# Half the columns of the second expert table read once as tiles instead of gathered row by row

## The chip, the cores and the metric

One core of one Trainium2 chip runs the whole program in one launch. The metric is the device time of that core in microseconds. A core has TensorE (PE), VectorE (DVE), ScalarE (ACT), GpSimd (POOL) and SyncE (SP), each with its own instruction queue, and 16 DMA engines that all queues share.

## The reference, cut to what matters

Two transformer blocks over 256 tokens of width 2048, in float32. The first and most of the second are products with weight matrices, attention and scans; the change leaves them as they are. It concerns the last layer, a mixture over 16384 single-row experts:

```python
def peer(x, w_q, sub_keys, expert_u, expert_v):      # tables: 16384 x 2048
    q = (x @ w_q).reshape(B, S, PEER_HEADS, 2, PEER_HALF)
    s = jnp.einsum('bshpk,hpnk->bshpn', q, sub_keys)  # 8 heads, 2 sides, 128 keys
    top_s, top_i = lax.top_k(s, PEER_TOPK)            # 16 of 128 on each side
    ...                                               # 16 best of the 16 x 16 sums
    ids = jnp.take_along_axis(cand_i, pos, axis=-1)   # first key * 128 + second key
    g = jax.nn.softmax(best_s, axis=-1)
    ...
        u = jnp.take(expert_u, it, axis=0)
        act = jax.nn.gelu(jnp.einsum('td,tkd->tk', xt, u)) * gt
        v = jnp.take(expert_v, it, axis=0)
        return jnp.einsum('tk,tkd->td', act, v)
```

So each token picks 8 x 16 = 128 experts. It needs 128 rows of the first table for 128 dot products, and 128 rows of the second, weighted and added. A last RMS norm follows.

## The kernel before, in words

Tokens lie on the 128 partitions, in two blocks t = 0 and 1. Up to about 2110 us weights stream through three buffers (`raw`): SP loads them, ACT makes a rounded copy (`wh`, line 1779), DVE the rest (`wl`, line 2222), and PE multiplies rounded parts (lines 1523 to 1536).

The expert phase numbers its work n = 0 to 255, where n = 128 t + k is pick k of every token in block t. For each n:

- POOL issues an indirect DMA of 128 rows of 8 KB, one for each token, from the first table into one of four buffers `Ub` (`get_u`, line 2784), once the dot that used the buffer is done;
- DVE multiplies the buffer with the normalised tokens `xn` and sums (`dot`, line 2656);
- after each four dots ACT applies gelu (`weigh`, line 2056) and DVE multiplies by the softmax weight (`weigh`, line 2663);
- POOL gathers 128 rows of the second table into one of twelve buffers `Vb` (`get_v`, line 2795);
- ACT builds a diagonal matrix of the 128 activations (`spread`, line 2064), and PE multiplies it with the rows and adds into four PSUM banks (`spread`, line 1685), in plain float32.

Between the dots DVE also chooses the experts of the 16 pairs (t, head): `top_sides`, `top_pairs`, `top_ids` and `top_weights` (lines 2598 to 2648). A planner, the class `Plan`, fixes the order of every engine's instructions before the program is written. It keeps one clock per engine, charges each piece of work an estimated time (`put`) and takes the option that could start first (`products`, line 881). It charges 2.55 us for a dot, 2.49 us of DMA for any gather, and 3.6, 2.4, 3.1 and 1.0 us for the four parts of a choice. Its order is then static: each engine runs its list in order and waits on semaphores. When the last rows are in, `finish` and `close` (lines 2675 and 2694) add the sums to the residual `X`, and normalise and store it.

Two queues matter for the change. POOL's holds the gathers in the planned order, so a gather that waits for its buffer holds those behind it. ACT's holds gelus and diagonals, and DVE's `weigh` waits for the gelu while all later dots stand behind it.

## Time and profile before

| | us |
|---|---|
| Median of three runs (lowest, highest) | 3402.46 (3401.48, 3403.65) |
| Profiled execution, first to last instruction (span) | 3401.7 |
| PE busy over the span | 3122.3 (92%) |
| DVE busy | 2242.8 (66%) |
| ACT busy | 1261.4 (37%) |
| POOL busy | 558.9 (16%) |
| HBM read | 931.5 MB |

The profiled execution has no time of its own beside its span; the span is 0.8 us below the median of the runs. Busy shares are means over stages with different limits, so the prediction reads stages. In the windows view, a row gives a stretch, its length, then for each engine the busy time and the number of instructions, then the granted TensorE clock, the mean busy share of the 16 DMA engines, and GB/s. A float32 product of PE shows as two records, a rounded one (float32r) as one.

### The profile page before, as it was taken

What the parts mean: (1) busy time and instruction counts of PE and PEld (TensorE: products, weight loads), DVE (VectorE), ACT (ScalarE), POOL (GpSimd) and SP (SyncE); (2) the same over time, 40 slices, a digit from 0 to 9 for tenths busy, and PEclk for the clock granted to TensorE, in tenths of its full rate; (3) what the DMA queues carried; (4) which work ended last, traced back from release to release, by engine and by line L of the source; (5) the groups of instructions that cost most, each with busy time, mean ns of one, the idle gap of its engine ahead of it and who ended that gap; (6) DMA issues with size and microseconds to landing.
All of it is one profiled execution on the core that took longest, in us unless ns stands there. A gap on an engine that the chain in (4) does not pass through costs nothing.

```text
span 3401.7 us, 35002 instructions
## 1 busy us (share of the span) xinstructions
PE 3122.3 (92%) x13582; PEld 2276.3 (67%) x13582; DVE 2242.8 (66%) x3449; ACT 1261.4 (37%) x1848; POOL 558.9 (16%) x533
## 2 busy tenths in 40 slices
PE   8999999999999999999999999999787777777776
PEld 7998998888888888888888888844232222222222
DVE  7786777775566877786557775888864454444445
ACT  6554566554445555554446763111110010000001
POOL 0000000000000000000000000664444343333333
PEclk9999999999999999999999999999999999999999
DMA  6554555546555555555556567999999999999998
GB/s 233 164 149 158 158 177 168 179 161 203 185 182 185 186 186 185 189 186 206 186 195 207 177 232 271 387 420 427 427 427 427 427 426 427 427 427 427 427 427 363
DMA packets 405597, 935.87 MB, mean 275 GB/s; under 512 B 16472, under 2 KB 246521, under 8 KB 339129
## 3 DMA queue, kind: packets, MB, share of 16 engines
q0 software_dynamic: 75936, 547.39, 38.4%
q1 hardware_dynamic: 328482, 385.92, 34.4%
q8 instruction: 107, 1.75, 0.2%
q10 hardware_dynamic: 1016, 0.35, 0.0%
q14 instruction: 56, 0.46, 0.0%
HBM read 931.50 MB, written 2.10 MB: 274 GB/s over the span
## 4 chain that ended last, share of the span: by engine, by line
PE 65%; DMA 27%; DVE 6%; issue 1%; ACT 1%; POOL 1%; POOLq 0%; DVEq 0%; SPq 0%; ACTq 0%
DMA Ub<-in_peer_u,ids 26%; PE W L1526 14%; PE W L1534 11%; PE W L1536 11%; PE W L1535 11%; PE W L1524 7%; DVE Ub L2656 4%; PE M L1685 2%; PE T L1685 2%; PE M L1587 1%; PE W L1460 1%; PE W L1523 1%; DMA Vb<-in_peer_v,ids 1%; POOL Vb L2795 0%; PE T L1421 0%
## 5 line engine op out<-in xcount | busy, mean ns | idle before, releaser
L2222 DVE TENSOR_TENSOR wl<-raw,wh 128x1024 fp32r<-128x1024 f32 (+1 forms) x720 | 850.6, 1186 | 563.5 <-ACT wh L1779 561.6
L1779 ACT ACTIVATE wh<-raw 128x1024 fp32r<-128x1024 f32 (+1 forms) x720 | 740.7, 1031 | 894.0 <-PE W L1536 573.6
L2656 DVE CUSTOM_DVE_ANT_0 Ub<-Ub,xn 128x2048 f32<-128x2048 f32 x256 | 585.6, 2291 | 480.9 <-DMA Ub<-in_peer_u,ids 480.9
L1526 PE MATMUL W<-u,wh 128*128 128x512 f32 x2040 | 722.7, 397 | 0.0
L1524 PE MATMUL W<-u,wl 128*128 128x256 f32 x2176 | 603.1, 282 | 0.2 <-DVE u L2184 0.2
L1685 PE MATMUL W<-Vb,diag 128*128 128x512 f32 x996 | 459.1, 603 | 156.7 <-DMA Vb<-in_peer_v,ids 154.2
L1685 PEld LDWEIGHTS W<-Vb,diag 128*128 128x128 f32 x996 | 179.4, 190 | 436.4 <-issue 373.8
L1526 PEld LDWEIGHTS W<-u,wh 128*128 128x128 f32 x2040 | 383.3, 188 | 88.4
L1534 PE MATMUL W<-wh,u 128*128 128x512 f32 (+1 forms) x1152 | 436.2, 379 | 1.2 <-DVE u L2582 1.0
L1536 PE MATMUL W<-wh,u 128*128 128x512 f32 (+1 forms) x1152 | 428.0, 371 | 0.0
L1535 PE MATMUL W<-wl,u 128*128 128x512 f32 (+1 forms) x1152 | 427.6, 371 | 0.0
L1524 PEld LDWEIGHTS W<-u,wl 128*128 128x128 f32 x2176 | 410.7, 189 | 6.4 <-issue 0.5
L2784 POOL DMA_INDIRECT Ub<-in_peer_u,ids x256 | 279.0, 1090 | 694.3 <-DVE dots L2656 588.0
L1685 PE MATMUL M<-Vb,diag 128*128 128x512 f32 x508 | 248.5, 612 | 95.5 <-DMA Vb<-in_peer_v,ids 93.1
L2056 ACT ACTIVATE dots<-dots 128x4 f32<-128x4 f32 x64 | 13.1, 205 | 782.6 <-DVE dots L2656 782.6
L2795 POOL DMA_INDIRECT Vb<-in_peer_v,ids x255 | 268.2, 1052 | 102.5 <-issue 71.0
L1685 PEld LDWEIGHTS M<-Vb,diag 128*128 128x128 f32 x508 | 91.2, 191 | 242.5 <-issue 209.0
L1685 PE MATMUL T<-Vb,diag 128*128 128x512 f32 x508 | 240.9, 597 | 0.0
L1534 PEld LDWEIGHTS W<-wh,u 128*128 128x128 f32 x1152 | 216.5, 188 | 30.5 <-issue 1.4
L1536 PEld LDWEIGHTS W<-wh,u 128*128 128x128 f32 x1152 | 216.2, 188 | 30.8
L1535 PEld LDWEIGHTS W<-wl,u 128*128 128x128 f32 x1152 | 216.6, 188 | 28.9
L1685 PEld LDWEIGHTS T<-Vb,diag 128*128 128x128 f32 x508 | 97.9, 193 | 124.3 <-issue 124.3
(371 smaller groups left out, 3265.0 us busy)
## 6 DMA issues: line engine op xcount, KB each, us to landing
raw<-in_w_in SPq DMA_DIRECT2D x128, 1024.0 KB, 5.2
raw<-in_w_up SPq DMA_DIRECT2D x88, 1024.0 KB, 4.8
raw<-in_w_down SPq DMA_DIRECT2D x44, 1024.0 KB, 4.9
raw<-in_w_in SPq DMA_DIRECT2D x144, 256.0 KB, 3.4
raw<-in_w_out SPq DMA_DIRECT2D x32, 1024.0 KB, 5.0
raw<-in_w_proj_a SPq DMA_DIRECT2D x16, 1024.0 KB, 4.9
Wb<-in_peer_w_q SPq DMA_DIRECT2D x16, 1024.0 KB, 7.7
raw<-in_w_proj_b SPq DMA_DIRECT2D x4, 1024.0 KB, 5.0
```

Of the source, the lines that this page charges most:

```text
L1460: m = q.matmul(pairs[n % 2][h][:, 0:T], w[:, k, col(h)], u5[:, kk, :], start=kk == 0, stop=kk == b.kt - 1)
L1524: i = q.matmul(pr[h][:, 0:T], vl, xh, start=False, stop=False)
L1526: i = q.matmul(o, vh, u[:, :, kk, :], start=False, stop=last)
L1534: q.matmul(o, th, H[:, k, :], start=first, stop=False)
L1535: q.matmul(o, th, L[:, k, :], start=False, stop=False)
L1536: i = q.matmul(o, tl, H[:, k, :], start=False, stop=last)
L1685: i = q.matmul(out_banks[t][j][:, :], diag[:, r % 4, :], v_row(n)[:, CK[j]], start=k == 0, stop=k == 127 or n == LAST_WHOLE and j > 1)
L1779: q.activation(wh[:, s % NS, 0:b.half], r, ACT.Copy).then_inc(s_hi, 1)
L2222: q.tensor_tensor(wl[:, s % NS, 0:b.half], r, wh[:, s % NS, 0:b.half].bitcast(F32), SUB).then_inc(s_lo, 1)
L2656: q.tensor_tensor_reduce(U[:, :], U[:, :], xn[:, t, :], 1.0, 0.0, MUL, ADD, dots[t][:, k:k + 1]).then_inc(s_dot, 1)
L2784: q.indirect_dma_start(Ub[place][:, :], None, eu, bass.IndirectOffsetOnAxis(ids[t][:, k:k + 1], 0)).then_inc(s_u[place], 16)
L2795: q.indirect_dma_start(v_row(n)[:, :], None, ev, bass.IndirectOffsetOnAxis(ids[t][:, k:k + 1], 0)).then_inc(s_v[n % NV], 16)
```

## The change

The second table's upper 1024 columns are still gathered row by row (half rows of 4 KB). Its lower 1024 columns are read once, in order, as 128 tiles of 128 experts x 1024 columns on SP's queue, and multiplied on PE by a matrix A of activations (experts x tokens), which is built on the chip.

- **Half gathers, block 0.** 128 gathers of upper halves (`get_v`), the first 72 through twelve places, the others through four, which lie where the scores were and wait for all choices. PE adds them by diagonals into two banks, as before.
- **Building A.** For each token, A[first key, second key] is the product of two one-hot matrices over its picks, the one weighted by the activations. Four tokens make a group; there are 32 groups for each block. `one_hot` and `spike` make the factors on ACT: an equality test against 0 to 127 is written as Abs (four operations of 128 columns), a wait, and Relu over 512 columns; the spike waits again and scales with four more. In block 1 every second spike is on DVE instead (four `tensor_scalar`). PE multiplies (`build`, four products of 128 columns), and ACT copies the bank to SBUF (`keep`). The groups of block 0 wait for all of its activations. The one-hots of block 1 follow, 28 of them at once and the last four after dot 235; its spikes wait for the activation of dot 239. The last 16 picks of block 1 are not in A.
- **The planner** gets an option "make" for these pieces, which is taken when ACT's clock plus 0.8 us is the earliest, and charges ACT 4.2 us for a one-hot with its spike, 0.6 for a keep, 1.5 for a one-hot alone and 2.3 for a spike alone. A dot from 240 on waits in the plan until a share of the spikes is placed. The first table has five buffers, of which four are in turn at a time (three from n = 236 on). A choice of experts is placed earlier than before where `eager` holds.
- **The products** (`dense`). For each tile j: ACT rounds the tile (`high`) and its 256 columns of A (one word in every 512 bytes for each token), DVE makes the rests (`low`, `low_a`), and PE does twelve rounded products of 512 columns. Each eleventh tile is multiplied in plain float32 with four products (`whole_tile`). Tiles have five buffers.
- **Aside.** Block 1's upper halves, and the lower halves of its last 16 picks, are 144 half gathers (`get_aside`, five buffers, not before the last dots), each added by DVE to `X` with one multiply-add of 1024 columns.
- The final norm's gain is multiplied in while the products run; both blocks close together.

The core of the diff (lists of places, semaphores and the closing steps are left out):

```diff
-NU = 4
-NV = 12
+NU = 5
 NW = 13
-LEAD = 7
 GROUP = 4
 LAG = 0.6
 
-ASIDE = (250, 252)
-HALVES = (253, 254, 255)
-SPREADS = [n for n in range(256) if n not in ASIDE]
-LAST_WHOLE = max(n for n in SPREADS if n not in HALVES)
+HALF = D // 2
+LATE = 16
+BUILT = 128 - LATE
+NE = 12
+NB = 4
+FIRST_ROWS = 72
+NT = 5
+NH = 3
+NA = 5
+ASIDES = 128 + LATE
+RAW = 11
...
+def row_place(m):
+
+    if m < FIRST_ROWS:
+        return m % NE, m // NE, m - NE if m >= NE else None
+    r = m - FIRST_ROWS
+    return NE + r % NB, r // NB, m - NB if r >= NB else None
...
+def whole_tile(j):
+    return j % RAW == RAW - 1
...
+    def build(self, i):
+
+        self.add("build", i)
+        self.put("PE", 1.0, max(self.clock["ACT"], self.clock["DVE"] if i % 2 and i > 32 else 0.0) + 0.2)
+        if i % 32:
+            self.keep(i - 1)
+
+    def keep(self, i):
+        self.add("keep", i)
+        self.put("ACT", 0.6, 0.0)
+
+    def make(self):
+
+        c = self.clock
+        yield lambda: None if 31 not in self.acted or FIRST_ROWS - 1 not in self.spreads else max(
+            self.acted[31], self.spreads[FIRST_ROWS - 1])
+        self.add("turn_ids", 0)
+        self.add("turn_act", 0)
+        self.put("ACT", 1.2, self.put("PE", 0.8, 0.0))
+        for i in range(32):
+            yield lambda: c["ACT"]
+            self.add("one_hot", i)
+            self.add("spike", i)
+            self.put("ACT", 4.2, 0.0)
+            self.build(i)
+        self.keep(31)
+        yield lambda: None if 124 not in self.dotted else self.when(("chosen", 1, 7), ("xn", 1, 3))
+        self.add("turn_ids", 1)
+        self.put("ACT", 0.6, self.put("PE", 0.6, 0.0))
+        for i in range(32, 64):
+            yield lambda: self.dotted.get(U_LAST[0]) if i >= 60 else c["ACT"]
+            self.add("one_hot", i)
+            self.put("ACT", 1.5, 0.0)
+        yield lambda: None if self.row_next < 128 else self.acted.get(BUILT // GROUP + 31)
+        self.add("turn_act", 1)
+        self.put("ACT", 0.6, self.put("PE", 0.4, 0.0))
+        for i in range(32, 64):
+            yield lambda: c["DVE"] if i % 2 else c["ACT"]
+            self.add("spike", i)
+            self.put("DVE" if i % 2 else "ACT", 0.8 if i % 2 else 2.3, 0.0)
+            self.build(i)
+            self.spiked = i - 31
+        self.keep(63)
...
+            eager = self.chosen < 3 + n / 9 and since > 0
+            if self.tasks and (dot is None or dot - c["DVE"] > 1.4 or 16 * self.chosen - u < 4 or eager):
+                options.append((c["DVE"] - (0.05 if eager else 0.0), "step"))
...
+            if want and want() is not None:
+                options.append((max(want(), c["ACT"]) + 0.8, "make"))
...
+    def dense(self):
+
+        for i in range(ASIDES):
+            self.add("get_aside", i)
+        a = 0
+        for j in range(128):
+            self.add("high", j)
+            self.add("low", j)
+            if j == 0:
+                self.add("rows")
+            while a < min(ASIDES, (j - 1) * ASIDES // 120):
+                self.add("aside", a)
+                a += 1
+            self.add("low_a", j)
+            self.add("mul", j)
+            if j % 4 == 3 and 7 <= j <= 19:
+                self.add("gain", (j - 7) // 4)
+            if j == 22:
+                self.add("upper", 0)
+        self.add("upper", 1)
+        self.add("close")
...
+            e.wait_ge(s_dot, 128)
+            q.dma_start(wide[:, :], cslice("wide")).then_inc(s_iota, 16)
+            gf_row = io["final_norm_g_2"].rearrange("(o d) -> o d", o=1)
+            e.wait_ge(s_spread, 128)
+            for j in range(128):
+                if j == 4:
+                    e.wait_ge(s_built, 64)
+                elif j > 4:
+                    e.wait_ge(s_taken, len(subs) + j - NT + 1)
+                q.dma_start(Vr[j % NT][:, :], ev[P * j:P * j + P, 0:HALF]).then_inc(s_whole[j % NT], 16)
...
+            def build(i):
+                t, g = group_of(i)
+                k = BUILT if t else P
+                e.wait_ge(s_hot, i + 1)
+                e.wait_ge(s_spa if on_act(i) else s_spd, spike_count(i))
+                e.wait_ge(*keeps(i))
+                for x in range(4):
+                    m = q.matmul((T0, T1)[i % 2][:, col(x)], A[t][0:k, 4 * g + x, :], spikes[i % 2][0:k, x, :], start=True, stop=True)
+                m.then_inc(s_built, 1)
+
+            def product(t, c, left, right, j, k):
+                return q.matmul(banks[f"W{2 * t + c}"][:, :], left, right, start=j == 0 and k == 0, stop=j == 127 and k == 2)
+
+            def mul(j):
+                if j == 0:
+                    e.wait_ge(s_turnk, 4)
+                a = j % 2
+                e.wait_ge(s_whole[j % NT], 32 + 16 * (j // NT + 1))
+                if whole_tile(j):
+                    e.wait_ge(s_ah, j + 1)
+                    for t in range(2):
+                        for c in range(2):
+                            m = product(t, c, Ar[a][:, t, :], Vr[j % NT][:, CK[c]], j, 1)
+                    m.then_inc(s_taken, 1)
+                    return
+                v = j - wholes(j) + 1
+                e.wait_ge(s_lo, plan.split_subs + v)
+                e.wait_ge(s_al, v)
+                H, L = Vh[(v - 1) % NH], Vl[j % NT]
...
+                for t in range(2):
+                    for c in range(2):
+                        product(t, c, Ah[a][:, t, :], H[:, CK[c]], j, 0)
+                    for c in range(2):
+                        product(t, c, Ah[a][:, t, :], L[:, CK[c]], j, 1)
+                    for c in range(2):
+                        m = product(t, c, Al[a][:, t, :], H[:, CK[c]], j, 2)
+                m.then_inc(s_taken, 1)
...
+            def peaks(out, k, t, j, g):
+
+                for x in range(4):
+                    s = 4 * g + x
+                    i = q.activation(out[0:k, x, :], wide[0:k, :], ACT.Abs, scale=-1.0, bias=idT[t][0:k, j, s:s + 1])
+                i.then_inc(s_act, me.up())
+                e.wait_ge(s_act, me.n)
+                return q.activation(out[0:k, :, :], out[0:k, :, :], ACT.Relu, scale=-1.0, bias=wide[0:k, 1:2])
...
+            def one_hot(i):
+                t, g = group_of(i)
+                e.wait_ge(s_iota, 32)
+                e.wait_ge(s_turnk, 2 * t + 1)
+                if t:
+                    e.wait_ge(s_gw, 16)
+                    e.wait_ge(s_dact, 32)
+                    e.wait_ge(s_xn, 8)
+                    e.wait_ge(s_smm, 9)
+                    e.wait_ge(s_dot, U_LAST[1] + 1)
+                    if g < 4:
+                        e.wait_ge(s_dot, U_LAST[0] + 1)
+                e.wait_ge(s_spread, FIRST_ROWS)
+                peaks(A[t][:, 4 * g:4 * g + 4, :], P, t, 1, g).then_inc(s_hot, 1)
...
+            def spike(i):
+                if not on_act(i):
+                    return
+                t, g = group_of(i)
+                k = BUILT if t else P
+                s = spikes[i % 2]
+                e.wait_ge(s_iota, 32)
+                e.wait_ge(s_turnk, 2 * t + 1)
+                e.wait_ge(s_turnk, 2 * t + 2)
+                if i >= 2:
+                    e.wait_ge(s_built, i - 1)
+                peaks(s, k, t, 0, g).then_inc(s_act, me.up())
+                e.wait_ge(s_act, me.n)
+                for x in range(4):
+                    o = q.activation(s[0:k, x, :], s[0:k, x, :], ACT.Copy, scale=actT[t][0:k, 4 * g + x:4 * g + x + 1])
+                o.then_inc(s_spa, 1)
+
...
+            def keep_group(i):
+                t, g = group_of(i)
+                bank, _ = keeps(i)
+                e.wait_ge(s_built, i + 1)
+                q.activation(A[t][:, 4 * g:4 * g + 4, :], (T0, T1)[i % 2][:, :].rearrange("p (x k) -> p x k", x=4),
+                             ACT.Copy).then_inc(bank, 1)
+
+            def high(j):
+                a = j % 2
+                both = strided(AA[:, j:j + 1], [(A1_o - A0_o) // 4, 2], [P, P])
+                if not whole_tile(j):
+                    v = j - wholes(j) + 1
+                    e.wait_ge(s_whole[j % NT], 32 + 16 * (j // NT + 1))
+                    if j == 0:
+                        e.wait_ge(s_dot, 256)
+                        e.wait_ge(s_built, 64)
+                    if v > NH:
+                        e.wait_ge(s_taken, len(subs) + last_high(v - NH) + 1)
+                    q.activation(Vh[(v - 1) % NH][:, :], Vr[j % NT][:, :], ACT.Copy).then_inc(s_hi, 1)
+                if j == 0:
+                    e.wait_ge(*keeps(64))
+                    e.wait_ge(*keeps(65))
+                if j >= 2:
+                    e.wait_ge(s_taken, len(subs) + j - 1)
+                q.activation((Ar if whole_tile(j) else Ah)[a][:, :, :], both, ACT.Copy).then_inc(s_ah, 1)
...
+            def low_v(j):
+                if j == 0:
+                    q.memset(ones[0:1, :], 1.0).then_inc(s_ones, 1)
+                if whole_tile(j):
+                    return
+                v = j - wholes(j) + 1
+                e.wait_ge(s_hi, plan.split_subs + v)
+                q.tensor_tensor(Vl[j % NT][:, :], Vr[j % NT][:, :], Vh[(v - 1) % NH][:, :].bitcast(F32), SUB).then_inc(s_lo, 1)
+
+            def low_a(j):
+                if whole_tile(j):
+                    return
+                both = strided(AA[:, j:j + 1], [(A1_o - A0_o) // 4, 2], [P, P])
+                e.wait_ge(s_ah, j + 1)
+                q.tensor_tensor(Al[j % 2][:, :, :], both, Ah[j % 2][:, :, :].bitcast(F32), SUB).then_inc(s_al, 1)
...
+            def aside(i):
+                k, upper_half = aside_of(i)
+                c = slice(HALF * upper_half, HALF * upper_half + HALF)
+                e.wait_ge(*landed("aside", i))
+                e.wait_ge(s_dact, 32 + k // GROUP + 1)
+                if i:
+                    e.wait_ge(s_aside, i)
+                q.scalar_tensor_tensor(X[:, 1, c], side_b[i % NA][:, :], dots[1][:, k:k + 1], X[:, 1, c], MUL, ADD).then_inc(s_aside, 1)
...
+            def get_v(m):
+                slot, _, before = row_place(m)
+                if m < len(EARLY):
+                    e.wait_ge(s_taken, chunk_used(EARLY[m]))
+                elif before is None:
+                    e.wait_ge(s_gw, 16)
+                    e.wait_ge(s_ids, 16)
+                else:
+                    e.wait_ge(s_spread, before + 1)
+                e.wait_ge(s_vid, m // 16 + 1)
+                q.indirect_dma_start(Vb[slot][:, :], None, ev_half,
+                                     bass.IndirectOffsetOnAxis(vid[0][:, m:m + 1], 0)).then_inc(s_place[LANDS["row", m][0]], 16)
+
+            def get_aside(i):
+                k, upper_half = aside_of(i)
+                if i < NA:
+                    e.wait_ge(s_spread, FIRST_ROWS)
+                    e.wait_ge(s_dot, U_LAST[side_place[i]] + 1)
+                else:
+                    e.wait_ge(s_aside, i - NA + 1)
+                e.wait_ge(s_vid, 8 + k // 16 + 1 if upper_half else 17)
+                index = vid[1][:, k:k + 1] if upper_half else vlow[:, k - BUILT:k - BUILT + 1]
+                q.indirect_dma_start(side_b[i % NA][:, :], None, ev_half, bass.IndirectOffsetOnAxis(index, 0)).then_inc(s_place[LANDS["aside", i][0]], 16)
```

## Rows read from the trace of the kernel before

**Rows 1.** Page, span in 40 equal slices of 85 us: busy tenths, and GB/s.

```profile
DVE  7786777775566877786557775888864454444445
GB/s 233 164 149 158 158 177 168 179 161 203 185 182 185 186 186 185 189 186 206 186 195 207 177 232 271 387 420 427 427 427 427 427 426 427 427 427 427 427 427 363
```

**Rows 2.** Windows: four stretches.

```profile
2200.00:2500.00 300.00, 270.91 (x622) 118.89 (x621) 253.05 (x615) 57.45 (x139) 153.28 (x125) 0.97 1.01 425
2500.00:3350.00 850.00, 634.47 (x1381) 248.55 (x1380) 409.73 (x402) 72.75 (x232) 328.06 (x345) 1.00 1.01 427
1600.00:1700.00 100.00, 100.00 (x451) 83.00 (x450) 56.82 (x60) 41.26 (x45) 0.00 (x0) 1.00 0.54 189
2210.00:2216.00 6.00, 4.58 (x11) 2.29 (x10) 5.54 (x5) 1.42 (x4) 5.39 (x3) 0.61 1.01 426
```

**Rows 3.** Waits, 2200 to 3402 us: total us, times, longest.

```profile
DVE Ub L2656 <- DMA Ub<-in_peer_u,ids: 463.0, 199, 3.5
```

**Rows 4.** Timeline of DVE: start us, us, engine line op, tiles, count, idle before.

```profile
2398.45 0.17 DVE L2644 TENSOR_TENSOR gw<-bs 128x16 f32<-128x16 f32 x1
...
2403.45 2.28 DVE L2656 CUSTOM_DVE_ANT_0 Ub<-Ub,xn 128x2048 f32<-128x2048 f32 x1
2405.66 0.08 DVE L2656 DVE_READ_ACCUMULATOR2_ANT dots<- 128x1 f32 x1
...
2408.69 0.42 DVE L2600 MAX8 bs<-cand 128x8 f32<-128x256 f32 x1
...
2411.07 2.27 DVE L2656 CUSTOM_DVE_ANT_0 Ub<-Ub,xn 128x2048 f32<-128x2048 f32 x1
2413.27 0.17 DVE L2626 TENSOR_SCALAR pi<-pos 128x16 uint32<-128x16 uint32 x1
...
2416.24 2.29 DVE L2656 CUSTOM_DVE_ANT_0 Ub<-Ub,xn 128x2048 f32<-128x2048 f32 x1
```

**Rows 5.** Lines 2656 and 2640, 2100 to 2200 us: ns min/median/max, first and last start.

```profile
L2656 DVE CUSTOM_DVE_ANT_0 Ub<-Ub,xn x23: 2282/2291/2312, 2115.2 to 2197.3; 128x2048 f32<-128x2048 f32 x23
L2640 DVE CAST ids<-sel x2: 174/175/176, 2109.1 to 2142.3; 128x16 uint32<-128x16 f32 x2
```

**Rows 6.** Gathers of the first table: landing times; POOL's timeline, one issue.

```profile
DMA to landing us min/median/max: 5.5/17.0/29.4
2153.68 2.75 POOL L2784 DMA_INDIRECT Ub<-in_peer_u,ids  x1 [3.85 <-DVE dots L2656]
```

**Rows 7.** ACT: timeline of three diagonals; two lines by source; DVE's weigh, groups by line.

```profile
3377.01 1.01 ACT L2064 ACTIVATE diag<-ident,dots 128x128 f32<-128x128 f32 x3
L2086 ACT ACTIVATE X<-xn,rstd x4: 705/714/723, 2794.2 to 3397.0; 128x512 f32<-128x512 f32 x4
L1809 ACT ACTIVATE XB<-W x8: 592/595/601, 583.8 to 758.7; 128x512 f32<-128x512 f32 x8
L2663 DVE TENSOR_TENSOR dots<-dots,gw 128x4 f32<-128x4 f32 x64 | 11.4, 178 | 22.2 <-ACT dots L2056 22.2
```

**Rows 8.** PE's timeline: rounded 512-column products; four plain 128-column ones (x8 records).

```profile
1603.05 0.39 PE L1536 MATMUL W<-wh,gl 128*128 128x512 f32 x1
1603.27 0.39 PE L1534 MATMUL W<-wh,gh 128*128 128x512 f32 x1
...
2209.48 1.16 PE L1661 MATMUL M<-kyT,qTt 128*128 128x128 f32 x8 [1.87 <-ACT qTt L1833]
```

**Rows 9.** DVE, groups by line and form: busy us, mean ns; one line by source.

```profile
L2437 DVE TENSOR_TENSOR E<-E,kb x64: 412/418/422, 68.2 to 746.8; 128x256 f32<-128x256 f32 x64
L2535 DVE TENSOR_TENSOR lt<-lt 128x1024 f32<-128x1024 f32 x4 | 4.9, 1218 | 0.0
L2703 DVE SCALAR_TENSOR_TENSOR X<-Vb,dots,X 128x512 f32<-128x512 f32 x6 | 4.2, 748 | 0.7 <-DMA Vb<-in_peer_v,ids 0.5
```

**Rows 10.** Timeline of the end: PE's last product, DVE's last operation.

```profile
3391.81 1.95 PE L1685 MATMUL W<-Vb,diag 128*128 128x512 f32 x4 [0.47 <-DMA Vb<-in_peer_v,ids]
3396.40 1.42 DVE L2728 SCALAR_TENSOR_TENSOR X<-X,rstd,gf 128x512 f32<-128x512 f32 x2
```

458 lines of the change are left out of this document (272 added, 186 removed).

## The prediction, as put on record before the change was run

> **What bounds the kernel now.** I read the slices first: in the first 23 the DMA engines move some 150 to 230 GB/s, and from slice 28 almost to the end 427, while DVE falls to four or five tenths [rows 1]. So the kernel has two halves. The weight streams, up to about 2110 us, are PE's and the change leaves them alone. The expert phase, about 1290 us, belongs to the gathers. Then the stages: from 2500 to 3350 us the DMA share is 1.01 and DVE is busy 410 of 850 us; from 2200 to 2500 us DMA is as full, but DVE is busy 253 of 300 us with the choice of experts beside the dots [rows 2]. Last the waits: the dot waits 463 us for its gather and for nothing else of size [rows 3]. A gather is 128 rows of 8 KB, 1.049 MB, so 2.46 us at 427 GB/s, and 512 of them make 1257 us. That is the bound.
>
> **What it removes.** Before, 268 + 268 MB are gathered. After: 268 MB of the first table; of the second, 128 half gathers for tokens 0 to 127 (67 MB), 144 halves "aside" for the others (75.5 MB) and 128 tiles read in order (67 MB). That is 478 MB, 59 MB less, worth 138 us at 427 GB/s. A row piece is now 4 KB. No row has that size: 2 KB pieces run at 189 GB/s with a DMA share of 0.54, so 350 GB/s if full; 8 KB pieces at 427 [rows 2]. With a fixed part per packet between these two, 4 KB comes to some 398 GB/s (my estimate; ends 350 and 427): a half gather or a tile takes 1.32 us (1.23 to 1.50). The saving shrinks to about 115 us. The question is what the new order loses, because work that ran side by side now stands in a row: all dots, then the rest of the matrix A, then the products.
>
> **Dots 24 to 70.** At 2200 us 23 dots and two heads' choices are done [rows 5], and the twelve rows fetched early are now halves, which lets the U gathers beside them come some 5 us sooner, so I start from 2195. One head costs DVE 5.0 (weights and sides) + 2.4 (pairs) + 3.0 (ids) = 10.4 us, and a dot 2.21 us [rows 4]. The planner still charges 2.49 us for a half row, so it expects idle DVE and lets the remaining thirteen and a half heads end near dot 70. DVE: 47 x 2.21 + 13.5 x 10.5 + 12 x 0.45 for weighing = 251 us. The bytes (47 U, 60 halves) need only 195, so DVE is the bound and DMA idles: 2446 us.
>
> **Dots 71 to 128** go one to one with the other 56 halves: 58 x 2.46 + 56 x 1.32 = 216 us of DMA; DVE needs 140. 2662 us. All of A(0) is still to be built, since it waits for the last activation of tokens 0 to 127.
>
> **Dots 129 to 240, beside ACT's building.** This is the step on which I forecast a loss. Three ACT operations on 128 columns with a column operand take 1.01 us together and 0.40 us alone, so one starts every 0.305 us; a 512 wide one with such an operand takes 0.71, one from PSUM 0.60 [rows 7]. One one_hot is four Abs and a Relu, with a wait between: 1.3 + 0.62 = 1.94 us. A spike adds another wait and four scaled copies: 3.25. A keep is 0.5. A group is 5.7 us, and 32 of them 182 us; the planner charges 4.2 + 0.6. The 28 one_hots of A(1) that follow are 54 us (charged 42). ACT would have room beside 112 dots of 2.46 us (275 us), if they were spread evenly. They are not: the planner puts a group whenever its ACT clock is behind (plus 0.8 us), so groups stand in ACT's queue ahead of the gelu of every four dots, and DVE's weigh waits for that gelu with all later dots behind it; those free the U buffers, so the gathers stop too. In the planner's time the 60 pieces take some 210 us, at about 2.9 us per dot with its stalls: 72 dots. On the chip these 72 take ACT's 182 + 54 + 18 x 0.3 + a few diagonals = 245 us, where DMA needs 177. The remaining 38 dots run at 2.46, or a little more, for a U ring holds four buffers and one gather takes 5.5 us to land at best; POOL's issue stretched to 2.75 us behind a dot [rows 6], so 2.5: 95 us. Dot 240 at 3002 us; between 2942 (no hold) and 3030.
>
> **The end of A(1).** 32 groups after dot 240: on ACT per pair one spike 3.25, two keeps 1.0, and 0.7 of waiting for the build just started (four 128-wide products take PE 1.16 us [rows 8]): 4.95 us. x16 = 79 us, + 2 for the transposes. DVE's spikes (0.8 us each) and the last 16 dots (35 us) fit beside it. 3083 us. DMA idles for half of this: 16 gathers and four tiles are 45 us, and the halves aside must wait for the U places until dot 253. If PE is at 1.2 GHz, as in part of 2210 to 2216 us, after it had idled (clock 0.61 in the mean) [rows 2], each pair costs 0.9 more.
>
> **The products.** Three chains of like length:
> - PE: rounded products of 512 columns start every 0.227 us [rows 8]; 117 tiles x 12 x 0.227 = 319, 11 whole tiles x 4 x 0.87 = 38 (two plain ones took PE 1.95 us to their end [rows 10]), the gain 3.5: 360 us.
> - DVE: a subtraction of 1024 columns is 1.22 us, less 0.07 overlap; one of 256 is 0.42, so 0.35; a multiply-add of 512 is 0.75, so about 1.28 for 1024, 1.22 in a row [rows 9]. 117 x 1.50 + 144 x 1.22 + 4 = 355 us, nearly all in the first 121 tiles; the last seven are PE's, so it ends at about 370.
> - DMA: 268 pieces x 1.32 = 354 us (330 to 402).
>
> With rings of five and three nearly full chains I take 373 us; 360 at best, 405 at worst. 3 us go to fill it. ACT has 1.3 us per tile and is no bound. 3459 us.
>
> **The close.** Before, the last product ended at 3393.8 and the span 7.9 us later [rows 10]. Now two token blocks close together: two more scalings on each engine: 10 us. SP's, POOL's and the loads' issues beside it: 144 + 128 + 256 gathers against 511 on POOL, no bound at about 1.24 us; the 128 tile loads are on SP, which is free. Removed with the change: PE's 128 + 126 spreads (free before, hidden by DMA), finish(0) (hidden). The sum is a span of 3469 us, against the profiled 3401.7; that span is 0.8 below the median of 3402.5, so I say **3470 us**, 2.0% slower.
>
> **Rivals.**
> 1. *Faster: ACT does not hold the dots.* It decides at dot 129 to 200: if ACT's queue holds less than about 9.8 us per four dots (1.6 groups), DMA keeps its pace. Then dot 240 is at 2662 + 112 x 2.5 = 2942, the tail 75, the products with their fill 361 and the close 10: **3388 us**. For it: ACT's total (240 us) does fit beside 275; against: the greedy rule, and 5.7 us instead of 4.8. With the early dots at DMA's pace too, 3335. Chance 0.30.
> 2. *The products are slower still.* low_a reads one word in every 512 bytes. The trace shows no cost of short strides: the products over halves, from single words to runs of 128, all take 0.41 to 0.42 us [rows 9]. If a long stride costs 0.18 us each, and DVE then is the longest chain, 117 x 0.18 = 21 us; if 4 KB pieces go as 2 KB ones, DMA needs 402. Either gives about **3495 us**. Chance 0.15. The Trainium skill, in Vector Engine (DVE) Microarchitecture Reference, section Measured stream behaviour on trn2, says that a port is at full rate only when its elements come in runs of two adjacent words, and gives 1.73 ns per column for one source that hops at every element; no run here shows this, and by it low_a would be some 0.18 us longer.
> 3. *The build at half clock.* PE is thin from dot 129 on; 0.9 us per pair, and slower spreads: **3490 us**. Chance 0.05.
> 4. *The halves do not halve.* If a gather cost by the row, 272 half gathers would cost as whole ones, and the products 500 us: 3600. Against it: pieces of 2 KB are far from four times slower. Chance 0.02.
>
> **How the numbers follow.** The forecast's own case has 0.48 (3430 to 3490 for itself). The range goes from 3370, which takes in rival 1, to 3520, with rivals 2 and 3. About 0.2% is what a measurement of this kernel can tell from no change. Rival 1 reaches faster with nearly all its 0.30; a mild hold lands within 0.2% with 0.05; the rest, 0.65, is slower.
>
> **What would show it.** Right: DVE waiting for ACT's gelu (now 22 us in all [rows 7]) rises past 60 us between dots 129 and 200; a DMA share well under 1 from 2200 to 2450 us, in that stretch, and for some 80 us before the products; a dot 240 near 3000 us; products at 2.9 us per tile. Wrong: DMA full to the last dot, or a last dot before 2990 us; a build of under 60 us; products below 360 us.

## The result and the profile after

The changed kernel takes 3605.7 us (median of four runs, 3603.8 to 3610.0) against 3402.2 us before it in the same comparison: **6.0% slower**, ratio 1.0601 [1.0588, 1.0614]. The prediction was 3470 us, range 3370 to 3520: the right side, but 136 us too little and outside the range.

From the page of the changed kernel, the slices and the bytes, which answer to [rows 1] (40 slices of 90.2 us here):

```profile
span 3608.2 us, 37732 instructions
PE 3024.2 (84%) x14084; PEld 2399.9 (67%) x14084; DVE 2611.8 (72%) x3896; ACT 1730.8 (48%) x2789; POOL 768.8 (21%) x549
...
DVE  7786777774567777765577668998855676369998
ACT  6555456554445555544467412211089701555555
...
PEclk9999999999999999999999999767667656679999
DMA  6554554565555555555564798899987899359997
GB/s 231 161 155 148 168 176 162 164 202 195 175 187 187 187 187 187 187 197 198 201 204 152 244 335 336 316 367 357 365 329 296 309 390 365 134 201 355 372 371 273
...
HBM read 872.84 MB, written 2.10 MB: 242 GB/s over the span
```

The slices of the weight streams look as before, and the bytes are 59 MB fewer, as forecast. After them the row of 427 GB/s is gone: about 300 to 390, and a hole in slices 35 and 36 (134 and 201). VectorE now has stretches of 8 and 9 tenths where it had 4 or 5, ScalarE of 7 to 9 where it had 0 or 1. The same by stage, cut at the events that the prediction names (on VectorE's timeline the 128th dot ends at 2619 us, the 240th at 3033):

```profile
core 0: us, PE busy (x) PEld busy (x) DVE busy (x) ACT busy (x) POOL busy (x), PEclk, DMA share, GB/s
2205.00:2620.00 415.00, 195.79 (x325) 72.04 (x323) 363.81 (x739) 70.36 (x163) 230.31 (x169) 0.73 0.92 344
2620.00:2880.00 260.00, 122.95 (x365) 70.83 (x365) 144.17 (x144) 240.45 (x665) 146.41 (x90) 0.68 0.80 309
2880.00:3033.00 153.00, 51.79 (x62) 17.23 (x60) 112.21 (x107) 13.91 (x45) 113.09 (x65) 0.58 0.97 381
3033.00:3097.00 64.00, 32.03 (x47) 12.10 (x45) 35.16 (x36) 4.03 (x15) 36.35 (x26) 0.74 0.92 349
3097.00:3191.00 94.00, 55.31 (x258) 50.92 (x256) 20.04 (x66) 68.00 (x177) 2.38 (x3) 0.61 0.08 26
3191.00:3597.00 406.00, 377.04 (x1499) 276.29 (x1500) 377.95 (x389) 206.87 (x258) 173.12 (x140) 0.99 0.92 344
```

Read it from the end. Products: 406 us, VectorE busy 378 of them. Ahead of them 94 us in which nothing is at its limit and DMA stands still (0.08): the second half of A is built alone. Ahead of that, 64 us in which ScalarE does next to nothing (4 us), though the build was due: the last rows of tokens 0 to 127 were still under way, and the transpose of the activations, with which the build begins, stands behind them in TensorE's list. And from 2620 to 2880 ScalarE is busy 240 of 260 us. The waits of 2620 to 2880, and then those of the products (engine, line, waited for, us in total, times, longest):

```profile
DVE dots L3007 <- ACT dots L2304: 112.1, 16, 10.9
```
```profile
POOL side L3159 <- DVE X L3051: 192.3, 112, 8.1
ACT Ah L2388 <- PE W L1895: 145.2, 108, 5.4
PEld W L1895 <- issue: 77.1, 168, 5.0
PE W L1895 <- DVE Al L3037: 29.2, 20, 4.8
```

112 us of VectorE waiting for a gelu, up to 10.9 us at a time: that is the hold of the forecast (22 us before, in all [rows 7]). In the products GpSimd and TensorE wait for VectorE, ScalarE for TensorE: it looks like VectorE's stage, which the experiments test. One group of A(0) on ScalarE's timeline (start, us, line), from the diagonal to the next:

```profile
2659.54 0.39 ACT L2310 ACTIVATE diag<-ident,dots 128x128 f32<-128x128 f32 x1
2659.83 1.27 ACT L2327 ACTIVATE AA<-wide,idT 128x128 f32<-128x128 f32 x4
2661.13 0.72 ACT L2330 ACTIVATE AA<-AA,wide 128x512 f32<-128x512 f32 x1
2661.76 1.26 ACT L2327 ACTIVATE spikes<-wide,idT 128x128 f32<-128x128 f32 x4
2663.05 0.72 ACT L2330 ACTIVATE spikes<-spikes,wide 128x512 f32<-128x512 f32 x1
2663.81 1.28 ACT L2361 ACTIVATE spikes<-spikes,actT 128x128 f32<-128x128 f32 x4
2664.99 0.57 ACT L2368 ACTIVATE AA<-T 128x512 f32<-128x512 f32 x1
2665.47 0.39 ACT L2310 ACTIVATE diag<-ident,dots 128x128 f32<-128x128 f32 x1
```

5.64 us from the start of the one_hot to the next diagonal, 5.93 from diagonal to diagonal: the forecast had 5.7.

### The profile page after: what moved, and what is told of

It is laid out like the page before. It is cut to its first block, busy times and chain, and to the rows that moved or that the text cites. A ratio compares the mean times of both kernels' runs of the same rounds, so it can differ in the third digit from the quotient of the medians.

```text
span 3608.2 us, 37732 instructions
## 1 busy us (share of the span) xinstructions
PE 3024.2 (84%) x14084; PEld 2399.9 (67%) x14084; DVE 2611.8 (72%) x3896; ACT 1730.8 (48%) x2789; POOL 768.8 (21%) x549
## 4 chain that ended last, share of the span: by engine, by line
PE 65%; DVE 13%; DMA 8%; ACT 7%; issue 3%; POOL 3%; DVEq 0%; SPq 0%; ACTq 0%; POOLq 0%
PE W L1715 13%; PE W L1723 11%; PE W L1725 11%; PE W L1724 11%; PE W L1713 7%; DMA Ub<-in_peer_u,ids 5%; DVE Ub L3000 5%; PE W L1895 4%; DVE X L3051 2%; POOL Ub L3135 2%; PE W L1649 2%; ACT AA L2327 2%; DMA Vr<-in_peer_v 2%; PE T L1891 2%; DVE Vl L3030 1%
## 5 line engine op out<-in xcount | busy, mean ns | idle before, releaser
L1862 PE MATMUL M<-Vb,diag 128*128 128x512 f32 x512 | 348.7, 831 | 398.9 <-DMA Vb<-in_peer_v,vid 355.9
L1862 PEld LDWEIGHTS M<-Vb,diag 128*128 128x128 f32 x512 | 124.5, 263 | 604.2 <-issue 535.4
L3135 POOL DMA_INDIRECT Ub<-in_peer_u,ids x256 | 419.0, 1637 | 439.3 <-DVE dots L3000 303.8
L3159 POOL DMA_INDIRECT side<-in_peer_v,vid x128 | 157.4, 1229 | 280.5 <-DVE X L3051 171.5
L1891 PE MATMUL T<-spikes,AA 128*128 128x128 f32 (+1 forms) x512 | 107.7, 386 | 128.1 <-issue 119.3
L1891 PEld LDWEIGHTS T<-spikes,AA 128*128 128x128 f32 (+1 forms) x512 | 96.5, 286 | 155.0 <-issue 155.0
L3051 DVE SCALAR_TENSOR_TENSOR X<-side,dots,X 128x1024 f32<-128x1024 f32 x144 | 184.3, 1280 | 2.5
L1895 PE MATMUL W<-Vh,Ah 128*128 128x512 f32 x468 | 156.4, 415 | 29.3 <-DVE Al L3037 29.2
```

The lines of the kernel that those rows point to most:

```text
L1862: i = q.matmul((M0, M1)[j][:, :], diag[:, m % 4, :], Vb[slot][:, CK[j]], start=m == 0, stop=m == 127)
L1891: m = q.matmul((T0, T1)[i % 2][:, col(x)], A[t][0:k, 4 * g + x, :], spikes[i % 2][0:k, x, :], start=True, stop=True)
L1895: return q.matmul(banks[f"W{2 * t + c}"][:, :], left, right, start=j == 0 and k == 0, stop=j == 127 and k == 2)
L3135: q.indirect_dma_start(Ub[place][:, :], None, eu, bass.IndirectOffsetOnAxis(ids[t][:, k:k + 1], 0)).then_inc(s_u[place], 16)
```

## The experiments

There are fifteen further kernels. Where no ratio is given there was one timed run, and the stage in its trace is the measure; four runs of one kernel lie up to 12 us apart here (e3's 31), so a few us in the time of a single run say nothing. "Stage of the products" is from the first to the last product on TensorE's timeline: 402 us in the changed kernel. The windows that begin at the 128th dot are cut one dot later in the experiments (end of the 129th to end of the 241st dot).

### Why the build starts so late

My first theory came from the planner: it charges a half gather with a whole one's 2.49 us and prefers gathers of the first table, so the last row of tokens 0 to 127 is asked for at 3086 us, beside dot 253, and A(1)'s first product, which needs all spreads done, cannot start before. The forecast had them done with dot 128. (A `put` books work on the planner's clock of an engine; `yield` says from when a piece may be placed.)

**e1, the half gather at its price.**
```diff
-        self.v_in[m] = self.put("DMA", 2.49, t + 1.2) + 1.5
+        self.v_in[m] = self.put("DMA", 1.3, t + 1.2) + 1.5
```


> The planner now charges 1.3 us of DMA for a half gather instead of 2.49; nothing else. In the changed kernel the last half row of block 0 is issued only at 3086 us, behind the gathers of the first table, and the build of A(1) starts at 3097, 64 us after dot 240; in this order the last half row stands after dot 204. Theory 1 (the half rows, late in the planned order, hold the build): the build starts within 10 us of dot 240, the last 16 dots run beside it, and the kernel takes 3535 to 3560 us instead of 3606. Theory 2 (ACT's groups and the bytes alone set the time; the rows come late because DMA is full anyway): dot 240 comes later by what the rows need, and the time stays above 3585.

**e2, e1 with the rows asked for first.**
```diff
-                options.append((max(v_free, c["DMA"] - 4.0), "v"))
+                options.append((max(v_free, c["DMA"] - 4.0) - 1.0, "v"))
```


> As the run before, and the planner prefers a half gather to one of the first table by 1 us, so that all half rows of block 0 are through near dot 137. Theory 1: the build starts at dot 240 as well, and the time is that of the run with the charge alone, 3530 to 3560 us. If the order of the rows matters more than the start of the build (four places, each freed by a product at half clock), this one is slower than that by over 15 us, since gathers of the first table wait on POOL behind half gathers whose place is not free.

**e3, e2 with ScalarE's true costs in the planner and its groups spread over the dots.**
```diff
-            yield lambda: c["ACT"]
+            yield lambda: self.dotted.get(128 + (5 * i) // 2)
...
-            self.put("ACT", 4.2, 0.0)
+            self.put("ACT", 5.2, 0.0)
...
-            yield lambda: self.dotted.get(U_LAST[0]) if i >= 60 else c["ACT"]
+            yield lambda: self.dotted.get(U_LAST[0] if i >= 60 else 208 + i - 32)
```


> As the run before, but the planner knows ACT's measured costs (5.2 us for a one-hot and a spike, 1.95 and 3.3 alone) and places the 32 groups of A(0) one for each 2.5 dots from dot 128 on, and the one-hots of A(1) one for each dot from 208. Theory (ACT's queue holds the dots, since weigh waits for a gelu behind the groups): dots 129 to 240 take 280 to 300 us instead of 414, DVE's wait for the gelu falls from 130 us to under 50, and the time falls another 40 to 70 us below the run with rows first, to 3470 to 3510. Rival (the half clock of PE or DMA's landing times pace these dots): less than 15 us change.

Measured: e1 3554.8 us (ratio 1.0461 [1.0444, 1.0479]), e2 3607.2 (1.0612 [1.0595, 1.0630]), e3 3570.1 (1.0511 [1.0470, 1.0552]). The stages of e1, and the one of e2 and of e3 in which dots 128 to 240 fall:

```profile
2205.00:2634.00 429.00, 168.27 (x334) 69.97 (x333) 367.15 (x741) 73.65 (x165) 274.11 (x172) 0.70 0.89 338
2634.00:3045.00 411.00, 167.62 (x462) 85.91 (x460) 257.79 (x256) 260.60 (x730) 257.05 (x161) 0.65 0.92 356
3045.00:3140.00 95.00, 55.68 (x257) 51.70 (x257) 53.81 (x100) 69.02 (x176) 16.86 (x18) 0.59 0.51 170
3140.00:3540.00 400.00, 376.56 (x1499) 275.76 (x1500) 374.25 (x383) 201.95 (x251) 180.46 (x139) 1.00 0.93 346
```
```profile
2693.00:3096.00 403.00, 95.08 (x351) 64.06 (x350) 258.17 (x256) 252.92 (x703) 242.71 (x135) 0.59 0.85 326
```
```profile
2698.00:3057.00 359.00, 106.21 (x348) 70.83 (x347) 260.78 (x256) 250.54 (x692) 245.86 (x132) 0.58 0.96 367
```

In e1 the build stands directly behind dot 240, with the last 16 dots beside it: the 64 us are gone, and 51 of them from the time. So the late rows cost that, and theory 1 held for e1. It failed for e2, which takes as long as the change (3607.2 us). There the last row is asked for behind dot 137, nearly the forecast's order: on GpSimd's timeline 106 rows have been issued when the 128th dot ends (79 in e1, 77 in the change). That dot then comes at 2685 us instead of 2631, and the dots behind it take as long as in e1 (403 against 411 us) with DMA at 0.85: while ScalarE holds the dots, there is too little left to transfer. In e3, with the groups spread, the same dots take 359 us at a share of 0.96, and VectorE's wait for the gelu between 2620 and 3100 us falls from 97 to 22 us. The hold is real, and rows asked for later are what fills it. But e3 had been expected at 280 to 300 us for these dots and at 3470 to 3510 us in all: it missed both, so the hold is not all that is slow there. Two stretches without much of it show this, 100 us of e7 (below), rich in rows, and 50 us of e2, in which no rows are left and ScalarE does nothing:

```profile
2700.00:2800.00 100.00, 67.61 (x204) 35.92 (x203) 88.14 (x133) 47.15 (x125) 84.75 (x51) 0.81 1.01 423
2950.00:3000.00 50.00, 0.00 (x0) 0.00 (x0) 42.54 (x43) 0.82 (x4) 42.80 (x19) 0.50 1.00 387
```

In the change and in ten versions (e1 to e3, e6, e7, e9 to e11, e14, e15) the last 40 dots before the 240th take 111 to 129 us, 2.8 to 3.2 us each, where the forecast had 2.5. What sets that, the ring of four buffers or GpSimd's issuing (42.8 of the 50 us), no run separated.

### What the hold costs

**e6, e1 with shorter groups** (one Abs and one Copy over 4 x 128 columns for four of each; the four positions of a group share one row number and one activation, so A(0) is another matrix):
```diff
-                for x in range(4):
+                for x in range(4) if t else (0,):
                     s = 4 * g + x
-                    i = q.activation(out[0:k, x, :], wide[0:k, :], ACT.Abs, ...)
+                    r = slice(x, x + 1) if t else slice(0, 4)
+                    i = q.activation(out[0:k, r, :], strided(wide[0:k, :], [0, 1 if t else 4], [1, P]), ACT.Abs, ...)
```


> The version with the half gather charged at 1.3 us (3554.8 us), and ScalarE's work on a group of A(0) made shorter: one Abs and one Copy over 4 x 128 columns in place of four of each over 128, so that the four positions of a group take the first one's row number and activation (the activation matrix is another than the reference's). A group falls from 5.7 to some 4.1 us. Theory, the dots 128 to 240 wait for gelus behind these groups: 32 x 1.6 = 51 us less of ScalarE, of which 30 to 50 us come out of the time, 3505 to 3525. Rival, the transfers bind there (their share was 0.92 in that stretch): less than 15 us, 3540 or more.

**e7, e1 with A(0)'s spikes on VectorE** (complete, with the change's result; the groups of A(0) are also spread, one to two dots, and A(1)'s one-hots one to a dot from dot 192):
```diff
-            return i < 32 or i % 2 == 0
+            return i >= 32 and i % 2 == 0
...
-            yield lambda: c["ACT"]
+            yield lambda: self.dotted.get(128 + 2 * i)
```


> A full version, same result as the change: the half gather charged at 1.3 us, and the 32 groups of spikes of A(0) made by VectorE's four compare-and-multiply (4 x 0.34 us) in place of ScalarE's four Abs, Relu and four Copies (3.3 us), one group to two dots from dot 128 on, the one-hots of A(1) one to a dot from dot 192. Theory, ScalarE's groups hold the dots: 105 us leave ScalarE, 44 us come to VectorE, which was busy 258 of 411 us there; dots 128 to 240 shrink from 411 to 375 us or so, where the transfers bind at some 390 GB/s: 3510 to 3530. Rival, VectorE's own chain of landing and dot sets that stretch: the 44 us are added and it is 3560 to 3600.

**e11, e7 with A(1)'s spikes on VectorE too:**
```diff
-            return i >= 32 and i % 2 == 0
+            return False
```


> The version with VectorE's spikes (3510.1 us), with the 32 groups of A(1) on VectorE too, where every second one was ScalarE's; same result. The stage from dot 240 to the first product took 95 us there: 16 pairs at 5.9 us. ScalarE falls from 4.5 to 1.2 us per pair, VectorE comes to 2 x 1.1 for spikes + 2.3 for the dot beside it. Theory, ScalarE's chain with TensorE sets the pace of that stage: it falls to 75 to 82 us and the time to 3490 to 3500. Rival, VectorE, now with spikes and dots in one line, waits on each build and landing and takes as long: within 5 us of 3510.

Measured: e6 3525.6 us, 29 below e1, just short of the 30 to 50 that were expected; e7 3510.1 (1.0313 [1.0296, 1.0330]), 45 below; e11 3489.9 (1.0252 [1.0235, 1.0269]), 20 below e7; both theories held. e6 is the clean test of the hold: it takes 51 us of work from ScalarE and leaves the order alone, and the time from the 128th to the 240th dot falls from 409 to 380 us. Dots 128 to 240 of e7 and, last line, the build beside the last dots in e11:

```profile
2637.00:3003.00 366.00, 175.25 (x462) 85.64 (x460) 294.75 (x386) 163.39 (x442) 273.85 (x161) 0.71 0.98 399
3003.00:3099.00 96.00, 56.49 (x257) 52.69 (x258) 54.16 (x102) 69.02 (x176) 16.85 (x18) 0.59 0.52 177
```
```profile
3007.00:3077.00 70.00, 49.17 (x244) 45.14 (x243) 68.22 (x160) 23.24 (x40) 17.63 (x18) 0.65 0.68 229
```

411 us became 366 although VectorE has 37 us more to do there. The spikes' move and the spreading of the groups are not told apart in these 45 us. DMA is now full in the first 210 us of the stretch (1.01 at 423 GB/s from 2700 to 2800, above) and 0.98 at 399 GB/s over all of it, so little of the hold is left. The build went from 96 to 70 us when its ScalarE chain was taken away; VectorE is busy 68 of the 70, and is its new limit.

### The half clock

**e10, the change with TensorE kept busy in the build:**
```diff
                 m.then_inc(s_built, 1)
+                if i > 32 and i % 2:
+                    for x in range(1):
+                        q.matmul(banks["W2"][:, :], ident[:, :], X[:, 0, CK[0]], start=True, stop=True)
```


> The change as it stands, with one more matmul on TensorE after every second group of the A(1) build: 128x512, of no use, into a bank that the products overwrite. It takes 0.9 us at full clock and 1.8 at half, and fits into the 2.3 us in which TensorE idles in each pair of groups. Theory, the build takes 94 us and not the forecast's 79 because TensorE does its groups at the half clock (granted 0.61): with the engine kept busy the clock rises and the build falls to 80 to 86 us, the time to 3592 to 3600. Rival, the clock stays or does not matter, since ScalarE's 4.5 us per pair set the pace: 94 us or more and 3606 or more.

Measured 3605.8 us, span 3604.0:
```profile
3097.00:3191.00 94.00, 60.67 (x296) 44.87 (x295) 25.45 (x75) 72.27 (x183) 3.78 (x3) 0.84 0.13 43
```
The clock rose from 0.61 to 0.84 and the stretch from the last spread to the first product shrank from 98 to 91 us; the time did not move by more than single runs differ. Neither theory as written: the higher clock gave some 7 us, net of what the added products cost TensorE between two groups; what the clock alone is worth stays open.

### What sets the products

**e4, the change with neighbouring words of A** (other parts of A enter the products):
```diff
-                both = strided(AA[:, j:j + 1], [(A1_o - A0_o) // 4, 2], [P, P])
+                both = strided(AA[:, j:j + 1], [(A1_o - A0_o) // 4, 2], [1, P])
```


> The changed kernel, but ACT and DVE read 128 neighbouring words of A for each block instead of one word in every 512 bytes; the products therefore take other parts of A than the reference does. Stride theory: low_a falls from 0.61 us to 0.42 and ACT's copy from 0.68 to about 0.40; the products, in which DVE is 93% busy, fall from 406 us by 117 x 0.19 = 22 us or a little more, to 375 to 386, and the time to about 3584. Rival (PE's and DMA's chains are as long): the products change by less than 8 us.

**e5, the multiply-adds of the asides 64 columns wide** (most of what the last rows add is left out):
```diff
-                q.scalar_tensor_tensor(X[:, 1, c], side_b[i % NA][:, :], dots[1][:, k:k + 1], X[:, 1, c], ...)
+                q.scalar_tensor_tensor(X[:, 1, c.start:c.start + 64], side_b[i % NA][:, 0:64], dots[1][:, k:k + 1], ...)
```


> The change as it stands, with the multiply-add of each row of the last tokens (1.28 us, 144 times) narrowed from 1024 to 64 columns, so that the kernel leaves out most of what the last 128 + 16 rows add. That takes some 0.9 us x 144, about 130 us, of VectorE's 378 busy us out of the 406 us of products. Theory, VectorE sets the pace of the products: the stage falls to what comes next, 380 to 390 us by the DMA share of 0.97 in its middle, and the time by 16 to 26 us from 3606. Rival, the transfers already set it: the stage stays within 5 us of 406, VectorE only waits more.

**e8, e4 and e5 together:**

> The change with both reliefs of the products stage: the narrowed multiply-adds (most of what the last rows add is left out) and the neighbouring words of A (another activation matrix than the reference's). VectorE falls to some 230 busy us of the stage, ScalarE to 170. Theory, with VectorE out of the way the transfers bind: the stage ends where the neighbouring words alone brought it, 385 to 390 us. Rival, TensorE binds: 1508 matmuls of which the full ones take 0.23 us, 360 to 368 us, and the time falls 20 to 30 us below the 3599 of the run with the neighbouring words alone.

**e9, e7 with more whole tiles:**
```diff
-RAW = 11
+RAW = 6
```


> The version with VectorE's spikes (3510.1 us) and every 6th tile of the second table multiplied whole in single precision in place of every 11th: 21 whole tiles, not 11, same result. A whole tile costs VectorE nothing in place of 1.22 + 0.61 us, and TensorE 8 x 0.45 in place of 12 x 0.227 us. Theory, VectorE sets the pace of the products (401 us, floor 367 us when it was relieved): 10 tiles x 1.83 = 18 us leave it, TensorE's floor rises by 9 us to 376: the stage takes 382 to 388 us, the time 3492 to 3498. Rival, ScalarE's copies or the transfers set it too: less than 8 us, 3502 or more.

Measured: e4 3599.1 us, stage 390; e5 3573.0, stage 368; e8 3572.3, stage 367; e9 3505.0 (1.0303 [1.0286, 1.0320]), stage 399 against 401 in e7. The price of the stride first, from the lines of the products, the change and then e4:

```profile
L2388 ACT ACTIVATE Ah<-AA 128x256 fp32r<-128x256 f32 x117 | 78.9, 674 | 146.1 <-PE W L1895 145.2 <-issue 0.6
L3037 DVE TENSOR_TENSOR Al<-AA,Ah 128x256 fp32r<-128x256 f32 x117 | 71.2, 609 | 6.0 <-ACT Ah L2388 5.7
```
```profile
L3037 DVE TENSOR_TENSOR Al<-AA,Ah 128x256 fp32r<-128x256 f32 x117 | 48.9, 418 | 4.9 <-ACT Ah L2388 4.8
L2388 ACT ACTIVATE Ah<-AA 128x256 fp32r<-128x256 f32 x115 | 48.1, 418 | 154.0 <-PE W L1895 152.4 <-issue 1.5
```

609 against 418 ns: 0.19 us each, 22 us of VectorE; of these 12 came out of the stage, less than the 20 to 31 expected and more than the rival's 8, so another chain is close behind. e5 came out 33 us faster where 16 to 26 had been expected, so VectorE's theory held, and with e8 no faster than e5 it is TensorE's 367 us that come next, as e8's rival had it; but e9, which takes 18 us from VectorE, gave 2, as its rival said. That needed two more tests and one of the order.

**e12, the low parts of the table 64 columns wide** (TensorE multiplies the high part once more in their place; what the low parts add is left out):
```diff
-                q.tensor_tensor(Vl[j % NT][:, :], Vr[j % NT][:, :], Vh[(v - 1) % NH][:, :].bitcast(F32), SUB).then_inc(s_lo, 1)
+                q.tensor_tensor(Vl[j % NT][:, 0:64], Vr[j % NT][:, 0:64], Vh[(v - 1) % NH][:, 0:64].bitcast(F32), SUB).then_inc(s_lo, 1)
```


> The change as it stands, with VectorE's low part of each split tile of the table narrowed from 1024 to 64 columns, and TensorE multiplying the high part in its place: what the low parts of the table add is left out. As many matmuls, as many transfers, the multiply-adds of the asides as wide as before; 117 x some 1.1 us = 130 us less of VectorE, as much as the narrowed asides took. Theory, VectorE's work in a line sets the pace of the products: the stage falls from 402 to 365 to 372 us as it did with the narrowed asides, the time to 3570 to 3577. Rival, it was the asides' own loop (five side tiles, each free only after its 1.28 us) or the pull of the wide multiply-adds on the transfers, for which ten tiles fewer to split gave nothing: the stage stays within 8 us of 402.

**e13, the asides gathered 64 columns wide:**
```diff
-                q.indirect_dma_start(side_b[i % NA][:, :], None, ev_half, ...)
+                width = HALF if i < NA else 64
+                source = ev_half if i < NA else ev.rearrange("n (a d) -> (n a) d", a=32)
+                q.indirect_dma_start(side_b[i % NA][:, 0:width], None, source, ...)
```


> The change as it stands, with all asides after the fifth gathered as 64 columns (of another place of the table) and not 1024; VectorE multiplies and adds as wide as before, on what lies in the tile, so the sums of the last 128 tokens are left wrong in what these rows add. 139 x 0.49 MB, 68 of the 143 MB of the stage, are left out. Theory VectorE: the stage stays at 395 to 402 us. Rival, the transfers (360 GB/s at a share of 0.97): the stage falls by 15 us or more.

**e14, e11 with the asides behind low_a on VectorE:**
```diff
+            self.add("low_a", j)
             while a < min(ASIDES, (j - 1) * ASIDES // 120):
                 self.add("aside", a)
                 a += 1
-            self.add("low_a", j)
```


> The version with all spikes on VectorE (3489.9 us), and in the products each tile's multiply-adds of the asides put behind its low part of A, not ahead of it, so that TensorE need not wait for them; same result. Theory, a TensorE that starts a tile 1.3 us earlier frees its tile buffer earlier, and the next load (7 us) and ScalarE's copy come earlier: the loop of five buffers loses a wait, the stage falls from 403 to 385 to 395 us and the time to 3472 to 3482. Rival, VectorE's sum of 374 busy us stays what it is and it only waits elsewhere: within 4 us of 3490.

**e15, e14 with RAW = 6:**

> The same with every 6th tile multiplied whole in place of every 11th, 18 us less of VectorE and 9 us more of TensorE. Ten tiles fewer to split gave 2 us of the stage where the asides stood ahead. Theory, that was because each tile then waited for the asides anyway: with them behind, the stage falls 8 to 15 us below that of the run before, 3460 to 3472. Rival, as then: within 3 us of the run before.

Measured: e12 3580.9 us, stage 373; e13 3609.8, stage 396; e14 3476.6 (1.0222 [1.0204, 1.0241]), stage 393 against 403 in e11; e15 3473.3 (1.0212 [1.0195, 1.0229]), stage 385. The products of e5 (with their middle), e12, e13, and of e15:

```profile
3192.00:3560.00 368.00, 365.06 (x1500) 281.93 (x1500) 244.39 (x384) 203.63 (x252) 146.01 (x139) 0.99 0.96 376
3250.00:3520.00 270.00, 267.28 (x1104) 206.38 (x1103) 180.11 (x288) 152.34 (x185) 119.25 (x114) 1.00 1.02 403
```
```profile
3195.00:3568.00 373.00, 365.45 (x1500) 280.59 (x1500) 269.50 (x382) 204.64 (x253) 182.21 (x139) 1.00 0.95 371
```
```profile
3201.00:3597.00 396.00, 376.38 (x1500) 275.78 (x1499) 374.08 (x383) 198.38 (x252) 176.90 (x139) 1.00 0.52 177
```
```profile
3075.00:3460.00 385.00, 376.93 (x1460) 273.22 (x1460) 359.46 (x364) 193.05 (x243) 236.82 (x140) 0.99 0.94 361
```

Relieved of 134 or 108 us, in either place (378 busy us down to 244 and 270), VectorE lets the stage fall to 368 and 373, and TensorE is then busy 99% and 98% of it. With half of the bytes gone (share 0.52) but VectorE as before, it stays at 396: the transfers are not the bound, though their share of 0.92 looked like it. e12 and e13 were expected so, to a us or so, and so was e14; e15's time is 1 us above its range. The order explains e9: with the multiply-adds of the asides ahead of low_a, TensorE waits for both. Put behind, the stage lost 10 us with not one instruction fewer, and now ten tiles fewer to split seem worth 8 us of it. That is not clear of noise: e15's median is 3 us below e14's, the runs of the two overlap, and each stage is read from one trace. The second half of e14's theory, that the loads then come earlier, I did not test by itself.

e15 is the best version found: 132 us faster than the change, 2.1% slower than the kernel before.

## Why the prediction was wrong

The terms of the sum against the trace of the change and of e2, in which the rows stand nearly where the forecast had them, in us:

| step | predicted | measured | e2 |
|---|---|---|---|
| dot 70 | 2446 | 2412 | 2434 |
| dot 128 | 2662 | 2619 | 2685 |
| dot 240 | 3002 | 3033 | 3091 |
| A(1)'s build starts | 3004 | 3097 | 3092 |
| its length | 79 | 94 | 95 |
| products with their fill | 376 | 406 | 405 |
| close | 10 | 11 | 11 |

- **What bounds the kernel, what is removed:** right, but for a wrong sum: by its own prices (256 x 2.46 + 400 x 1.32 us against 1257) the saving is 100 us, not 115; nothing was worked out from it. In the middle of e5's products, where half pieces run alone, DMA is full at 403 GB/s; the forecast's estimate was 398.
- **Dots 24 to 70:** 34 us too long. The choices do not end near dot 70 but at 2566 us, behind dot 110; 11 of the 16 are done at dot 70, so fewer of them stood in the way of the first 70 dots.
- **"Dots 71 to 128 go one to one with the other 56 halves" is the step that failed first.** When the 128th dot ends, 51 halves are still to be issued. Two things kept them back. The last 56 wait for all choices, and those end behind dot 110: on GpSimd's timeline the 73rd row is issued beside dot 112 in the change and in each of the ten versions named above. From there on only the halves for which the planner saw room went; they trailed to dot 253 at less than one in two dots. That flattered dot 128 (43 us early), put the rows into the next stage, and held the build 64 us after dot 240 where the forecast had 2. e1 takes that wait away: 51 us of the time. I had read the planner's charge of 2.49 us for the end of the choices, and not for the order of the rows themselves.
- **Dots 129 to 240 are the second step that failed.** The mechanism was right: 5.7 us per group, VectorE's wait for the gelu 112 us against the 60 that I had named as the sign, and ScalarE needs 251 us for the 60 pieces where I had 245. But beside them go 60 dots (56 in e2), not 72, and the 52 dots behind them take 3.1 us each (2.75 in e2, without rows), not 2.5. The forecast also counted 38 of these where 112 less 72 are 40, 5 us. So the stage took 414 us, not 340, and 406 in e2, with 22 rows in it instead of 42: it is long without the rows that moved here. e6 and e7, which shorten the hold, give back 29 and 46 us of it; what sets the slow dots behind it stays open. e2 also says that the late rows alone do not explain the miss. With the rows nearly as forecast the kernel is as slow, and the 134 us by which its span exceeds the forecast's are 23 (dot 128), 66 (this stage), 16 (build), 29 (products) and the rest. **Rival 1**, "ACT does not hold the dots", is false; and with the hold shortened e7 still has its 240th dot at 2998 us, not at 2942.
- **The end of A(1):** 94 us against 79. Its price was in **rival 3**, 0.9 us per pair at half clock, 15 us. The clock was at 0.61, and nearly all of the 15 us is waiting: ScalarE's work is the forecast's (68 us), but it waits 24.6 us in all for TensorE's groups, 0.8 to 1.7 a pair, where I had 11. In e10, at 0.84, it waits 17.2: about half of what was missing came back. e11, with the spikes off ScalarE, shows that its chain with TensorE sets the pace.
- **The products:** TensorE's 360 us (365 measured when it set the pace) and the transfers' 354 were fair. VectorE's 355 was mis-sized: 378. That is **rival 2**: "if a long stride costs 0.18 us each" it costs 21 us; it was 0.19 and 22. On the trace of before I could only say that short strides are free [rows 9]. By the Trainium skill, Vector Engine (DVE) Microarchitecture Reference, section Measured stream behaviour on trn2, one source that hops 4 KiB at every element runs at 1.73 ns per column. The hops here are of 512 bytes, and of that figure only the difference to neighbouring words, 0.18 us by the prediction's estimate, agrees with the 609 against 418 ns. Of the 30 us by which the stage is too long, the stride gave back 12 (e4) and the order on VectorE, at which the forecast did not look, 10 in another version (e14); the rest stays open.
- **Rival 4**, the halves do not halve: false, by the 403 GB/s of the half pieces alone in e5.

31 us (dot 240) + 62 (late rows) + 15 (build) + 30 (products) + 1 (close) = 139, the distance from the forecast span of 3469 to 3608. The late rows alone would have passed the upper end of the range, which lay 50 us above; and that dot 128 came 43 us early is luck in the sum, for it is the same rows. The chance for the forecast's own case was too high for a sum in which three new stages stand in a row, each priced at the pace of its busiest engine.

Why a kernel with 12% fewer bytes in this phase is slower at all: before, DMA was full for 1185 us (2205 to 3390 us, share 1.01, 425 GB/s). Now 446 MB, which at the old 425 GB/s would need 1049 us, lie in 1392 us, in stages in which another engine holds it: VectorE's choices and dots, ScalarE's groups, the build, the products. e15 has cut that to 1255 us.

## What to carry to other kernels

Bytes saved count only where the transfers stay full: when work is moved from one stream into stages, price the joints (what must be finished before the next stage may start) as well as the stages. Where a planner orders the work, change its charge for every operation whose size changes, and read from its own clocks where it will put them. Build the order that the forecast assumed, as e2 did: where it is as slow, the step found first is not the only one. A DMA share of 0.9 does not say that DMA is the bound: take bytes away and look.
